# Turning gated operands and block queries in 32x32 squares on VectorE and through DRAM, instead of on TensorE

## The chip, the cores and the metric

The kernel runs on one core of one Trainium2 chip. The metric is device time in microseconds (us) of one execution; lower is better. TensorE (PE in the profile) multiplies matrices, VectorE (DVE), ScalarE (ACT) and GpSimd (POOL) work on elements, and SyncE (SP) issues nearly all DMA transfers. SBUF and PSUM are the memories on the chip, DRAM the one beside it.

## The reference

One decoder block in float32 over 256 tokens of width 1024. A projection gives the inputs of two groups of four heads each: gated linear attention (GLA) and block attention (MoBA, called block attention here). Both are followed by one output projection, a SwiGLU network and a norm.

```python
h = rms_norm(x, norm1_gain[l])
proj = h @ w_in[l]                    # gq, gk, gv, gr, g_low, mq, mk, mv
...
q_dec = q * jnp.exp(b); k_inv = k * jnp.exp(-b)        # b: running sum of log gates
a = jnp.where(causal, jnp.einsum('bhncd,bhnsd->bhncs', q_dec, k_inv), 0.0)
...                                   # intra-chunk part, state part
q_m = rotary(to_heads(mq, MOBA_HEADS), positions)
k_m = rotary(to_heads(mk, MOBA_HEADS), positions)
o_moba = moba_attention(q_m, k_m, to_heads(mv, MOBA_HEADS))
x = x + jnp.concatenate([o_gla, o_moba], axis=-1) @ w_out[l]
h = rms_norm(x, norm2_gain[l])
x = x + (jax.nn.silu(h @ w_ffn_gate[l]) * (h @ w_ffn_up[l])) @ w_ffn_down[l]
return rms_norm(x, final_norm_gain)
```

With 256 tokens there is one key block, so block attention is causal attention here. Scores need queries and keys with the head dimension on the partitions, while the projection delivers them with tokens on the partitions: they have to be turned.

## The kernel before

**Units.** The weights come in units of 128x2048 float32 (1 MB, two DMAs of 512 KB on SP's queue) into a ring of three raw buffers. Each unit is split into a high and a low part: ScalarE's `split` rounds raw to `w_hi` (L858), VectorE's `split` subtracts (`w_lo`, L1072). TensorE multiplies three times (hi*hi, lo*hi, hi*lo; L471 to L473), 24 matrix products of 512 columns for each unit. Units 0 to 11 are the input projection, two for each block of columns: 0, 1 GLA queries and keys; 2, 3 block queries; 4, 5 block keys; 6, 7 block values; 8, 9 GLA values; 10, 11 the output gate. Units 12 to 15 are the output projection, the rest the network.

**What sets the order.** Everything is written out by hand, engine by engine, with semaphores; every engine runs its own list in order. SP loads unit u into the raw buffer only when VectorE has split unit u - 3 (`raw_free`), so VectorE's splits pace the loads. ScalarE's `split(u)` waits for the landing of unit u, VectorE's for ScalarE's, TensorE for both (`unit_ready`).

**The small steps.** TensorE's list puts the attention steps between the halves of the units (`midway`) or behind them (`after`):

```python
midway = {2: [logits], 7: [lambda: moba_transposed(1)],
          9: [probs_transposed], 10: [moba_outputs, gla_updates], 11: [lambda: heads_transposed(0, (3, 0)), gla_outputs]}
after = {3: [cumulate], 4: [gla_transposed],
         6: [gla_scores, lambda: moba_transposed(0)], 7: [moba_scores]}
```

- `gla_transposed` (L576, reading `reuse_c`): ten 128x128 transposes of the gated operands after unit 4. ScalarE copies PSUM to `qdT`, `kiT`, `qcT` (L926 to L930), VectorE the other half of `qdT` (L1191). `gla_scores` (L626) after unit 6 reads them.
- `moba_transposed(0)` and `(1)` (L576, reading `reuse_e`): eight transposes each, of the rotated block queries (after unit 6) and keys (in the middle of unit 7). Copies: ScalarE L935 and L940, VectorE L1194 and L1208. `moba_scores` (L636, L640) after unit 7 reads them.
- VectorE: gates multiply the operands (L1180 to L1185), `split(6)`, `split(7)`, `rotate(0)` (six operations, L1170 to L1175), `split(8)`, a copy, `rotate(1)`, a copy, `split(9)`, four masked copies of GLA scores (L1203), a copy, `split(10)`, the row maxima of the block scores (L1212 to L1222), `split(11)`, `split(12)`.
- ScalarE: `take_block(1)` (L875, block queries out of PSUM), `split(8)`, three copies, `split(9)`, `take_block(2)` (keys; it overwrites what `rotate(0)` reads, so it waits for `rotated` 1), a copy, `split(10)`, `split(11)`, a copy, `split(12)`, `take_block(3)` (values), the eight exponentials of the softmax (L948), a table load (L951), `split(13)`. `probs_transposed` in the middle of unit 9 waits for the exponentials.

## Time and profile before

| | us |
|---|---|
| median of 3 runs (305.68 to 305.84) | 305.72 |
| the profiled execution's own time | 305.38 |
| its span, first to last instruction | 303.7 |
| PE busy in the span | 296.2 |
| DVE busy | 231.7 |
| ACT busy | 153.7 |

The page gives busy time by engine, the granted clock of TensorE, the chain that ended last, the costliest groups and the DMA issues. In a timeline a line is: start in us, duration in us, engine, line of the kernel, operation, out<-in, size of an operand, count, and in brackets the idle time of the engine before it with what released it. Several like instructions in a row are merged into one line (x8). Durations of neighbours on one engine overlap by some tens of ns, so the step from start to start is what an instruction takes in a row of others. Engine SPq is SyncE's queue of DMA issues.

### The profile page before, as it was taken

Reading aid. Unit: us, or ns where it says so; the run is one execution under the profiler, and the core shown is the slowest. Engines: PE = TensorE matmul, PEld = TensorE weight load, DVE = VectorE, ACT = ScalarE, POOL = GpSimd, SP = SyncE. Lnnn points to the kernel's source line nnn. Section 1 sums busy time; section 2 is a strip of 40 time slices with the busy share of each in tenths; the row PEclk is TensorE's granted clock in tenths of the full one; section 3 lists DMA queues with packets and bytes.
Section 4 is the critical chain, followed back from the end, with each engine's and each line's share of the span. In section 5 each row is a group of like instructions: output and inputs, shape, how many; then the busy total and the mean of one; then the engine's idle time right before and its main releaser. Section 6 shows DMA issues by size and latency. Waiting matters only on the chain.

```text
span 303.7 us, 4006 instructions
## 1 busy us (share of the span) xinstructions
PE 296.2 (98%) x1407; PEld 247.1 (81%) x1407; DVE 231.7 (76%) x375; ACT 153.7 (51%) x189; POOL 21.9 (7%) x42
## 2 busy tenths in 40 slices
PE   8999999999999999999999999999999999999992
PEld 7788888888888888888888888888888888888881
DVE  1999999996487257679797979797878878787155
ACT  2898994699363527326262626262617071713123
POOL 6050100000112001500000000000000000000011
PEclk9999999999999999999999999999999999999998
DMA  7987856337825303914747474747472919030003
GB/s 233 359 294 254 276 200 218 138 141 276 276 86 192 138 2 92 316 77 156 262 158 259 159 255 158 256 163 252 139 276 82 331 34 368 19 133 0 0 2 138
DMA packets 36599, 54.42 MB, mean 179 GB/s; under 512 B 2870, under 2 KB 25962, under 8 KB 36586
## 3 DMA queue, kind: packets, MB, share of 16 engines
q1 hardware_dynamic: 36420, 54.08, 52.1%
q8 instruction: 8, 0.13, 0.2%
q10 hardware_dynamic: 166, 0.17, 0.2%
q14 instruction: 5, 0.04, 0.0%
HBM read 53.19 MB, written 1.05 MB: 179 GB/s over the span
## 4 chain that ended last, share of the span: by engine, by line
PE 94%; DMA 2%; DVE 1%; issue 1%; POOL 1%; ACT 0%; SPq 0%; POOLq 0%; DVEq 0%
PE acc L471 15%; PE acc L473 14%; PE acc L472 14%; PE aux L471 13%; PE aux L472 13%; PE aux L473 13%; PE aux L576 3%; DMA raw<-in_w_in 2%; PE acc L525 1%; PE acc L528 1%; PE acc L531 1%; PE aux L658 1%; DVE x_sb L1285 1%; PE aux L682 1%; PE aux L640 1%
## 5 line engine op out<-in xcount | busy, mean ns | idle before, releaser
L1072 DVE TENSOR_TENSOR w_lo<-raw,w_hi 128x2048 fp32r<-128x2048 f32 x47 | 105.6, 2287 | 11.3 <-ACT w_hi L858 11.2
L858 ACT CAST w_hi<-raw 128x2048 fp32r<-128x2048 f32 x47 | 87.7, 1907 | 6.9 <-DMA raw<-in_w_out 3.3
L471 PE MATMUL aux<-w_hi,aT_hi 128*128 128x512 f32 (+1 forms) x180 | 69.8, 388 | 0.0
L473 PE MATMUL aux<-w_hi,aT_lo 128*128 128x512 f32 (+1 forms) x180 | 69.6, 387 | 0.0
L472 PE MATMUL aux<-w_lo,aT_hi 128*128 128x512 f32 (+1 forms) x180 | 69.6, 387 | 0.0
L1321 DVE STREAM_TRANSPOSE reuse_c<-reuse_c 32x128 f32<-32x128 f32 x160 | 48.4, 303 | 2.4
L471 PE MATMUL acc<-w_hi,aT_hi 128*128 128x512 f32 x118 | 47.3, 401 | 0.0
L473 PE MATMUL acc<-w_hi,aT_lo 128*128 128x512 f32 x118 | 46.1, 391 | 0.0
L472 PE MATMUL acc<-w_lo,aT_hi 128*128 128x512 f32 x118 | 46.0, 390 | 0.0
L473 PEld LDWEIGHTS aux<-w_hi,aT_lo 128*128 128x128 f32 x180 | 33.8, 188 | 6.9
L471 PEld LDWEIGHTS aux<-w_hi,aT_hi 128*128 128x128 f32 x180 | 33.8, 188 | 6.9
L472 PEld LDWEIGHTS aux<-w_lo,aT_hi 128*128 128x128 f32 x180 | 33.8, 188 | 6.7
L1015 ACT CAST pT_hi<-reuse_c 128x512 fp32r<-128x512 f32 x10 | 6.2, 621 | 64.7 <-DVE reuse_c L1321 64.7
L471 PE MATMUL acc<-w_hi,pT_hi 128*128 128x512 f32 x80 | 31.2, 390 | 0.0
L473 PE MATMUL acc<-w_hi,pT_lo 128*128 128x512 f32 x80 | 31.1, 389 | 0.0
L472 PE MATMUL acc<-w_lo,pT_hi 128*128 128x512 f32 x80 | 31.1, 389 | 0.0
L1002 ACT ACTIVATE reuse_c<-aux,rstd 128x256 f32<-128x256 f32 x22 | 10.2, 472 | 32.4 <-PE aux L473 32.3
L473 PEld LDWEIGHTS acc<-w_hi,aT_lo 128*128 128x128 f32 x118 | 22.2, 188 | 4.8
L471 PEld LDWEIGHTS acc<-w_hi,aT_hi 128*128 128x128 f32 x118 | 22.2, 188 | 4.4 <-issue 0.2
L472 PEld LDWEIGHTS acc<-w_lo,aT_hi 128*128 128x128 f32 x118 | 22.2, 188 | 4.3
L1311 DVE SCALAR_TENSOR_TENSOR reuse_c<-aux,rstd,reuse_c 128x256 f32<-128x256 f32 x22 | 10.2, 480 | 13.2 <-ACT reuse_c L1002 13.2
L473 PEld LDWEIGHTS acc<-w_hi,pT_lo 128*128 128x128 f32 x80 | 15.0, 188 | 3.2
(199 smaller groups left out, 272.1 us busy)
## 6 DMA issues: line engine op xcount, KB each, us to landing
raw<-in_w_ffn_gate SPq DMA_DIRECT2D x22, 512.0 KB, 4.2
raw<-in_w_ffn_up SPq DMA_DIRECT2D x22, 512.0 KB, 5.3
raw<-in_w_ffn_down SPq DMA_DIRECT2D x22, 512.0 KB, 5.7
raw<-in_w_in SPq DMA_DIRECT2D x20, 512.0 KB, 4.7
raw<-in_w_out SPq DMA_DIRECT2D x8, 512.0 KB, 3.9
raw<-in_w_in SPq DMA_DIRECT2D x8, 256.0 KB, 6.2
x_sb<-in_x SPq DMA_DIRECT2D x2, 512.0 KB, 3.9
reuse_a<-in_final_norm_gain SPq DMA_DIRECT2D x1, 512.0 KB, 4.3
```

Of the source, the lines that this page charges most:

```text
L471: nc.tensor.matmul(dst, left_hi[:, k, tok], right_hi, start=first, stop=False)
L472: nc.tensor.matmul(dst, left_hi[:, k, tok], right_lo, start=False, stop=False)
L473: return nc.tensor.matmul(dst, left_lo[:, k, tok], right_hi, start=False, stop=last)
L525: nc.tensor.matmul(acc[:, t, :], aT_hi[:, k, toks[t]], right_hi, start=k == 0, stop=False)
L528: nc.tensor.matmul(acc[:, t, :], aT_hi[:, k, toks[t]], right_lo, start=False, stop=False)
L576: last = nc.tensor.transpose(aux[:, bank, n * P:(n + 1) * P], src, ident[:, :])
L858: nc.scalar.copy(w_hi[:, slot % RING, :], raw[:, slot % RAW, :]).then_inc(hi_ready, 1)
L1002: nc.scalar.activation(silu_g[:, t, :], aux[:, GATE_UP_BANKS[parity][t], 0:FF], ACT.Silu, scale=rstd[:, 1, t:t + 1]).then_inc(silu_ready, 1)
L1015: nc.scalar.copy(dst, src.rearrange("p (k s) -> p k s", k=2)).then_inc(hiddenT_hi_ready, 1)
L1072: nc.vector.tensor_tensor(w_lo[:, slot % RING, :], raw[:, slot % RAW, :], w_hi[:, slot % RING, :].bitcast(f32), ALU.subtract).then_inc(lo_ ...
L1311: nc.vector.scalar_tensor_tensor(out=hidden[:, t, :], in0=aux[:, GATE_UP_BANKS[parity][t], FF:2 * FF], scalar=rstd[:, 1, t:t + 1], in1=sil ...
L1321: last = nc.vector.transpose(cols[SQUARE * c:SQUARE * (c + 1), :, :, g, :], rows[SQUARE * g:SQUARE * (g + 1), :, :, c, :])
```

## The change

The ten transposes of the GLA operands and the eight of the block queries leave TensorE; the eight of the block keys stay. In their place VectorE turns all 32x32 squares of a group in one instruction (`nc.vector.transpose`: 128x1280 for GLA, 128x1024 for the block queries) into a buffer of squares. SP writes the squares to a DRAM scratch (one DMA each, 640 KB and 512 KB), waits for it to land, and reads them back with four DMAs each, one for each group of 32 partitions, so that the squares arrive at their place. GLA queries are used where they land (`gla_columns`); ScalarE copies the other GLA operands to `kT` and the block queries to `mT_q`, so that they lie in contiguous columns. The orders change too: on VectorE the turn of the GLA operands comes before `split(6)`, the turn of the block queries and `rotate(1)` before `split(8)`, and `split(9)` behind the masked copies and the copy of the keys; on ScalarE `take_block(2)` comes before `split(9)`, the copy to `kT` behind it, the copy to `mT_q` behind `split(10)`; on SP the waits and DMAs of the two moves stand between the loads of units 8 and 11. The semaphores' declarations and two like lists are left out of the diff.

```diff
@@ -52,7 +52,9 @@
 SQUARE = 32
-QUADS = 4
+QUADS = P // SQUARE
+GLA_TILES = 4 * PAIRS + PAIRS
+MOBA_TILES = T * HEADS
 X2T_BANKS = (0, 3, 1, 2)
...
@@ -139,9 +141,8 @@
         lowT = sb("lowT", [SEQ])
-        qdT = sb("qdT", [PAIRS, 2, SEQ])
-        kiT = sb("kiT", [PAIRS, SEQ])
-        qcT = sb("qcT", [PAIRS, P])
+        gla_columns = sb("gla_columns", [QUADS, GLA_TILES, SQUARE])
+        kT = sb("kT", [3 * PAIRS, P])
         state = sb("state", [HEADS, DV])
...
@@ -178,7 +179,9 @@
         q_mid, k_mid = (reuse_c[:, 512 * i:512 * i + 512].rearrange("p (t n) -> p t n", t=T) for i in range(2))
-        k_end, q_cum = (reuse_c[:, 1024 + QK * i:1024 + QK * (i + 1)] for i in range(2))
+        q_cum, k_end = (reuse_c[:, 1024 + QK * i:1024 + QK * (i + 1)] for i in range(2))
+        gla_rows = reuse_c[:, 0:GLA_TILES * P].rearrange("p (n c i) -> p c n i", c=QUADS, i=SQUARE)
+        gla_squares = reuse_f[:, 0:GLA_TILES * P].rearrange("p (c n i) -> p c n i", c=QUADS, i=SQUARE)
         squares = reuse_c[:, 0:1024]
...
@@ -190,7 +193,11 @@
         s_1 = reuse_e[:, 512:1536].rearrange("p (h k) -> p h k", h=HEADS)
-        mT = reuse_f[:, :].rearrange("p (w h s) -> p w h s", w=2, h=HEADS)
+        m_columns = reuse_f[:, 0:1024].rearrange("p (c n i) -> p c n i", c=QUADS, i=SQUARE)
+        mT_q = reuse_a[:, :].rearrange("p (t h s) -> p t h s", t=T, h=HEADS)
+        mT_k = reuse_f[:, 1024:2048].rearrange("p (h s) -> p h s", h=HEADS)
+        m_rows = reuse_e[:, 0:1024].rearrange("p (n c i) -> p c n i", c=QUADS, i=SQUARE)
+        m_squares = reuse_c[:, 0:1024].rearrange("p (c n i) -> p c n i", c=QUADS, i=SQUARE)
         probT = reuse_f[:, 0:1536].rearrange("p (b h q) -> p b h q", b=3, h=HEADS)
...
@@ -301,6 +313,9 @@
+        gla_moves = nc.dram_tensor("gla_moves", (P, QUADS, GLA_TILES * SQUARE), f32).ap()
+        m_moves = nc.dram_tensor("m_moves", (P, QUADS, MOBA_TILES * SQUARE), f32).ap()
+
         block = ctx.enter_context(nc.Block())
@@ -355,9 +370,29 @@
             sp.dma_start(gate_bias, b_gate.to_broadcast([P, QK])).then_inc(bias_loaded, 16)
-            for u in range(RAW, IN_UNITS):
-                raw_free(u)
-                rows_unit(u % RAW, w_in[0], (u % 2) * 4 * P, 4, BLOCKS[u // 2], 512)
+            def in_units(lo, hi):
+                for u in range(lo, hi):
+                    raw_free(u)
+                    rows_unit(u % RAW, w_in[0], (u % 2) * 4 * P, 4, BLOCKS[u // 2], 512)
+
+            def squares_out(ready, n, moves, squares, moved):
+                sp.wait_ge(ready, n)
+                sp.dma_start(moves, squares.rearrange("p c n i -> p c (n i)")).then_inc(moved, 16)
+
+            def columns_back(moved, moves, columns, landed):
+                sp.wait_ge(moved, 16)
+                for c in range(QUADS):
+                    sp.dma_start(columns[SQUARE * c:SQUARE * (c + 1)].rearrange("p g n i -> p g (n i)"),
+                                 moves[:, c, :].rearrange("(g j) n -> j g n", g=QUADS)).then_inc(landed, 16)
+
+            in_units(RAW, 9)
+            squares_out(gla_squares_ready, 1, gla_moves, gla_squares, gla_moved_out)
+            in_units(9, 10)
+            columns_back(gla_moved_out, gla_moves, gla_columns, gla_columns_back)
+            in_units(10, 11)
+            squares_out(m_squares_ready, 1, m_moves, m_squares, m_moved_out)
+            columns_back(m_moved_out, m_moves, m_columns, m_columns_back)
+            in_units(11, IN_UNITS)
             for n in range(OUT_UNITS):
...
@@ -405,7 +440,6 @@
             nc.gpsimd.memset(one[:, :], 1.0)
-            nc.gpsimd.memset(qdT[:, :, :, :], 0.0)
             nc.gpsimd.memset(state[:, :, :], 0.0)
...
@@ -590,55 +624,44 @@
                 for t, tri in enumerate((tri_rest, tri_cum)):
-                    cols = slice(t * QK, (t + 1) * QK)
-                    nc.tensor.matmul(aux[:, 3, cols], tri[:, :], log_hi[:, cols], start=True, stop=False)
-                    last = nc.tensor.matmul(aux[:, 3, cols], tri[:, :], log_lo[:, cols], start=False, stop=True)
+                    cols, dst = slice(t * QK, (t + 1) * QK), slice((1 - t) * QK, (2 - t) * QK)
+                    nc.tensor.matmul(aux[:, 3, dst], tri[:, :], log_hi[:, cols], start=True, stop=False)
+                    last = nc.tensor.matmul(aux[:, 3, dst], tri[:, :], log_lo[:, cols], start=False, stop=True)
                 last.then_inc(cum_in_psum, 1)
-            def gla_transposed():
-                pe.wait_ge(gla_ops_ready, 3)
-                for bank, src in ((1, q_mid), (2, k_mid)):
-                    transposes(bank, [src[:, t, pair * P:(pair + 1) * P] for pair in range(PAIRS)
-                                      for t in range(T)]).then_inc(glaT_in_psum, 1)
-                transposes(0, [q_cum[:, pair * P:(pair + 1) * P] for pair in range(PAIRS)]).then_inc(glaT_in_psum, 1)
-
-            def moba_transposed(which):
-                pe.wait_ge(rotated, which + 1)
-                if which == 0:
-                    pe.wait_ge(glaT_by_act, 3)
-                else:
-                    pe.wait_ge(mT_by_act, 1)
-                    pe.wait_ge(mT_by_dve, 1)
+            def moba_k_transposed():
+                pe.wait_ge(rotated, 2)
                 for n, bank in enumerate((3, 0)):
-                    transposes(bank, [m_rot[:, which, t, h, :] for h in (2 * n, 2 * n + 1)
+                    transposes(bank, [m_rot[:, 1, t, h, :] for h in (2 * n, 2 * n + 1)
                                       for t in range(T)]).then_inc(mT_in_psum, 1)
...
-                pe.wait_ge(glaT_by_act, 2)
-                pe.wait_ge(glaT_by_dve, 1)
+                pe.wait_ge(gla_columns_back, 16 * QUADS)
+                pe.wait_ge(kT_ready, 1)
                 for t in range(T):
-                    tok = slice(t * P, (t + 1) * P)
                     for pair in range(PAIRS):
...
                             rows = slice(par * DK, (par + 1) * DK)
-                            last = nc.tensor.matmul(aux[:, 1 + par, col:col + P], kiT[rows, pair, tok],
-                                                    qdT[rows, pair, par, tok], start=True, stop=True)
+                            n = t * PAIRS + pair
+                            last = nc.tensor.matmul(aux[:, 1 + par, col:col + P], kT[rows, n, :],
+                                                    gla_columns[rows, :, n, :], start=True, stop=True)
                 last.then_inc(a_in_psum, 1)
...
-                pe.wait_ge(mT_by_act, 2)
-                pe.wait_ge(mT_by_dve, 2)
+                pe.wait_ge(mT_q_ready, 1)
+                pe.wait_ge(mT_by_act, 1)
+                pe.wait_ge(mT_by_dve, 1)
                 pe.wait_ge(a_ready, 2)
                 for h in range(HEADS):
-                    last = nc.tensor.matmul(aux[:, 1, h * P:(h + 1) * P], mT[:, 0, h, 0:P], mT[:, 1, h, 0:P],
+                    last = nc.tensor.matmul(aux[:, 1, h * P:(h + 1) * P], mT_q[:, 0, h, :], mT_k[:, h, 0:P],
                                             start=True, stop=True)
...
                 for h in range(HEADS):
-                    last = nc.tensor.matmul(aux[:, 2 + h // 2, (h % 2) * SEQ:(h % 2 + 1) * SEQ], mT[:, 0, h, P:SEQ],
-                                            mT[:, 1, h, :], start=True, stop=True)
+                    last = nc.tensor.matmul(aux[:, 2 + h // 2, (h % 2) * SEQ:(h % 2 + 1) * SEQ], mT_q[:, 1, h, :],
+                                            mT_k[:, h, :], start=True, stop=True)
                     if h % 2:
...
@@ -682,7 +705,7 @@
                         if t:
-                            last = nc.tensor.matmul(aux[:, 1 + t, cols], qcT[:, h // 2, :], state[:, h, :],
+                            last = nc.tensor.matmul(aux[:, 1 + t, cols], kT[:, 2 * PAIRS + h // 2, :], state[:, h, :],
                                                     start=False, stop=True)
...
@@ -765,10 +788,9 @@
-            midway = {2: [logits], 7: [lambda: moba_transposed(1)],
+            midway = {2: [logits], 7: [moba_k_transposed],
                       9: [probs_transposed], 10: [moba_outputs, gla_updates], 11: [lambda: heads_transposed(0, (3, 0)), gla_outputs]}
-            after = {3: [cumulate], 4: [gla_transposed],
-                     6: [gla_scores, lambda: moba_transposed(0)], 7: [moba_scores]}
+            after = {3: [cumulate], 6: [gla_scores], 7: [moba_scores]}
             for k in range(KC):
...
@@ -922,22 +944,20 @@
             split(8)
-            act.wait_ge(glaT_in_psum, 1)
-            nc.scalar.copy(qdT[0:DK, :, 0, :], aux[0:DK, 1, :].rearrange("p (a s) -> p a s", a=PAIRS)).then_inc(glaT_by_act, 1)
-            act.wait_ge(glaT_in_psum, 2)
-            nc.scalar.copy(kiT[:, :, :], aux[:, 2, :].rearrange("p (a s) -> p a s", a=PAIRS)).then_inc(glaT_by_act, 1)
-            act.wait_ge(glaT_in_psum, 3)
-            nc.scalar.copy(qcT[:, :, :], aux[:, 0, 0:PAIRS * P].rearrange("p (a s) -> p a s", a=PAIRS)).then_inc(glaT_by_act, 1)
-            split(9)
             act.wait_ge(rotated, 1)
             take_block(2, m_flat)
+            split(9)
+            act.wait_ge(gla_columns_back, 16 * QUADS)
+            nc.scalar.copy(kT[:, :, :].rearrange("p n (g i) -> p n g i", g=QUADS),
+                           gla_columns[:, :, 2 * PAIRS:GLA_TILES, :].rearrange("p g n i -> p n g i")).then_inc(kT_ready, 1)
+            split(10)
+            act.wait_ge(m_columns_back, 16 * QUADS)
+            nc.scalar.copy(mT_q.rearrange("p t h (g i) -> p (t h) g i", g=QUADS),
+                           m_columns.rearrange("p g n i -> p n g i")).then_inc(mT_q_ready, 1)
+            act.wait_ge(rotated, 2)
             act.wait_ge(mT_in_psum, 1)
-            nc.scalar.copy(mT[:, 0, 0:2, :], aux[:, 3, :].rearrange("p (h s) -> p h s", h=2)).then_inc(mT_by_act, 1)
-            split(10)
+            nc.scalar.copy(mT_k[:, 0:2, :], aux[:, 3, :].rearrange("p (h s) -> p h s", h=2)).then_inc(mT_by_act, 1)
             split(11)
-            act.wait_ge(rotated, 2)
-            act.wait_ge(mT_in_psum, 3)
-            nc.scalar.copy(mT[:, 1, 0:2, :], aux[:, 3, :].rearrange("p (h s) -> p h s", h=2)).then_inc(mT_by_act, 1)
             split(12)
...
@@ -1183,16 +1203,15 @@
             nc.vector.tensor_tensor(k_end, gqk[:, 0, QK:2 * QK], k_end, ALU.mult).then_inc(gla_ops_ready, 1)
+            dve.wait_ge(gla_ops_ready, 3)
+            nc.vector.transpose(gla_squares, gla_rows).then_inc(gla_squares_ready, 1)
             split(6)
...
             rotate(0)
+            dve.wait_ge(rotated, 1)
+            nc.vector.transpose(m_squares, m_rows).then_inc(m_squares_ready, 1)
+            rotate(1)
             split(8)
-            dve.wait_ge(glaT_in_psum, 1)
-            nc.vector.tensor_copy(qdT[DK:P, :, 1, :], aux[DK:P, 1, :].rearrange("p (a s) -> p a s", a=PAIRS)).then_inc(glaT_by_dve, 1)
-            rotate(1)
-            dve.wait_ge(mT_in_psum, 2)
-            nc.vector.tensor_copy(mT[:, 0, 2:4, :], aux[:, 0, :].rearrange("p (h s) -> p h s", h=2)).then_inc(mT_by_dve, 1)
-            split(9)
...
@@ -1204,8 +1223,9 @@
                 last.then_inc(a_ready, 1)
-            dve.wait_ge(mT_in_psum, 4)
-            nc.vector.tensor_copy(mT[:, 1, 2:4, :], aux[:, 0, :].rearrange("p (h s) -> p h s", h=2)).then_inc(mT_by_dve, 1)
+            dve.wait_ge(mT_in_psum, 2)
+            nc.vector.tensor_copy(mT_k[:, 2:4, :], aux[:, 0, :].rearrange("p (h s) -> p h s", h=2)).then_inc(mT_by_dve, 1)
+            split(9)
             split(10)
...
```

## Rows read from the trace of the kernel before

**Rows 1.** The page: busy time by engine, and the chain that ended last.

```profile
PE 296.2 (98%) x1407; PEld 247.1 (81%) x1407; DVE 231.7 (76%) x375; ACT 153.7 (51%) x189; POOL 21.9 (7%) x42
...
PE 94%; DMA 2%; DVE 1%; issue 1%; POOL 1%; ACT 0%; SPq 0%; POOLq 0%; DVEq 0%
```

**Rows 2.** Timeline of TensorE around unit 4's end: start, us, instruction.

```profile
39.26 0.40 PE L473 MATMUL acc<-w_hi,aT_lo 128*128 128x512 f32 x1
39.50 1.25 PE L576 MATMUL aux<-ident,reuse_c 128*128 128x128 f32 x10
40.51 0.48 PE L471 MATMUL acc<-w_hi,aT_hi 128*128 128x512 f32 x1
40.82 0.39 PE L472 MATMUL acc<-w_lo,aT_hi 128*128 128x512 f32 x1
```

**Rows 3.** Timeline of TensorE from the GLA scores to unit 9's middle.

```profile
51.59 1.16 PE L626 MATMUL aux<-qdT,kiT 64*128 64x128 f32 x16
52.69 1.09 PE L576 MATMUL aux<-ident,reuse_e 128*128 128x128 f32 x8
53.53 0.48 PE L471 MATMUL acc<-w_hi,aT_hi 128*128 128x512 f32 x1
...
56.40 1.04 PE L576 MATMUL aux<-ident,reuse_e 128*128 128x128 f32 x8
...
60.01 1.05 PE L636 MATMUL aux<-reuse_f 128*128 128x128 f32 x8
...
62.44 0.58 PE L471 MATMUL acc<-w_hi,aT_hi 128*128 128x512 f32 x1
...
70.83 1.47 PE L576 MATMUL aux<-ident,reuse_e 128*128 128x128 f32 x12
```

**Rows 4.** Timeline of VectorE, 37 to 66 us.

```profile
37.76 4.49 DVE L1072 TENSOR_TENSOR w_lo<-raw,w_hi 128x2048 fp32r<-128x2048 f32 x2
42.18 0.69 DVE L1170 TENSOR_TENSOR reuse_e<-reuse_d,cos_t 128x512 f32<-128x512 f32 x1
...
46.18 2.28 DVE L1072 TENSOR_TENSOR w_lo<-raw,w_hi 128x2048 fp32r<-128x2048 f32 x1
...
54.42 2.28 DVE L1072 TENSOR_TENSOR w_lo<-raw,w_hi 128x2048 fp32r<-128x2048 f32 x1
56.62 1.44 DVE L1203 COPY_PREDICATED reuse_b<-gla_mask,aux 128x256 f32<-128x256 int32 x4
57.95 0.68 DVE L1208 COPY reuse_f<-aux 128x512 f32<-128x512 f32 x1
...
61.10 0.69 DVE L1212 TENSOR_TENSOR reuse_e<-aux,causal 128x512 f32<-128x512 f32 x1 [0.27 <-PE aux L636]
...
65.27 4.49 DVE L1072 TENSOR_TENSOR w_lo<-raw,w_hi 128x2048 fp32r<-128x2048 f32 x2
```

**Rows 5.** Timeline of ScalarE, 47 to 68 us.

```profile
47.40 1.26 ACT L875 ACTIVATE reuse_d<-acc,rstd 128x512 f32<-128x512 f32 x2
...
61.39 1.90 ACT L858 CAST w_hi<-raw 128x2048 fp32r<-128x2048 f32 x1 [3.33 <-DMA raw<-in_w_out]
...
64.35 0.40 ACT L948 ACTIVATE reuse_e<-reuse_e,neg_max 128x128 f32<-128x128 f32 x1
...
67.98 1.28 ACT L951 ACT_TABLE_LOAD   x1
```

**Rows 6.** Timeline of SyncE's DMA issues: the load of unit 12.

```profile
56.73 0.82 SPq L320 DMA_DIRECT2D raw<-in_w_out  x2
```

**Rows 7.** Page: the 32x32 transposes. Columns: busy us, mean ns.

```profile
L1321 DVE STREAM_TRANSPOSE reuse_c<-reuse_c 32x128 f32<-32x128 f32 x160 | 48.4, 303 | 2.4
```

**Rows 8.** Groups by shape on VectorE, 30 to 75 us.

```profile
L1116 DVE SCALAR_TENSOR_TENSOR reuse_e<-reuse_e 128x128 f32<-128x128 f32 x3 | 0.9, 293 | 0.1
```

**Rows 9.** DMA issues: count, KB each, median us from issue to landing.

```profile
out<-reuse_e ACTq DMA_DIRECT2D x1, 160.0 KB, 2.3
```

**Rows 10.** Busy time, clock, DMA share and GB/s of one microsecond.

```profile
43.00:44.00 1.00, 1.00 (x6) 0.83 (x5) 1.00 (x2) 1.00 (x2) 0.00 (x0) 1.00 1.04 401
```

More of the change, by code:

```diff
@@ L253, in build_block @@
         gla_ops_ready = sem("gla_ops_ready")
-        glaT_in_psum = sem("glaT_in_psum")
-        glaT_by_act = sem("glaT_by_act")
-        glaT_by_dve = sem("glaT_by_dve")
+        gla_squares_ready = sem("gla_squares_ready")
+        gla_moved_out = sem("gla_moved_out")
+        gla_columns_back = sem("gla_columns_back")
+        kT_ready = sem("kT_ready")
+        m_squares_ready = sem("m_squares_ready")
+        m_moved_out = sem("m_moved_out")
+        m_columns_back = sem("m_columns_back")
+        mT_q_ready = sem("mT_q_ready")
         mT_in_psum = sem("mT_in_psum")
```

## The prediction, made before the changed kernel was run

> **What bounds the kernel now.** I read the page first: TensorE is busy for 98% of the span, and 94% of the chain that ended last is TensorE's [rows 1]. So TensorE's own list is the critical path, and any transpose taken from it counts in full unless something new makes TensorE wait. Then I read TensorE's timeline through the attention steps, from start to start [rows 2, 3]: there is no gap. Then the timelines of the engines that feed it. VectorE runs without a pause from 37.76 us through `split(9)` to the row maxima [rows 4]: at this place the second engine is full too, and its splits release SP's loads. ScalarE's exponentials run from 64.35 to 67.98 us [rows 5], and TensorE transposes their result at 70.83 us [rows 3]: 2.85 us of slack. That slack, and how much work the change puts on VectorE ahead of `split(9)`, is what the forecast turns on.
>
> **What is removed from TensorE.** The ten transposes after unit 4 start at 39.50 us and unit 5 at 40.51 us, and the first product behind them takes 0.31 us to the next start instead of 0.23: 1.01 + 0.08 = 1.09 us [rows 2]. The eight transposes of the block queries take 53.53 - 52.69 = 0.84 us [rows 3]. Together 1.93 us, from 18 of 26 transposes; the eight of the keys stay. The scores themselves read other tiles at the same sizes: nothing.
>
> **VectorE's new list.** A transpose of 128 elements per partition takes 303 ns [rows 7]. No row shows one of 1280. Lower value: an ordinary operation takes 293 ns at 128 elements [rows 8] and 2280 at 2048 [rows 4], so 1.04 ns for each further element; 303 + 1152 x 1.04 = 1.50 us for GLA and 303 + 896 x 1.04 = 1.24 us for the block queries. Upper value: ten and eight times 303 ns, 3.03 and 2.42 us. I take the lower: a slope twice as steep would leave some 40 ns of fixed cost for the 128-element transpose, and its duration is within 10 ns of the ordinary operation's. Nothing supports less than the slope of the other operations, so there is no end below. The Trainium skill ("Vector Engine (DVE) Microarchitecture Reference", section 3.8) states of the transpose mode that it is "Pipelined to sustain one element per cycle per lane"; by that the two together are about the 2.74 us taken, against 5.45 us by the upper value, and the row of 303 ns agrees with it as far as it goes.
>
> The list then runs so, with steps from rows 4. The GLA turn 37.76 to 39.26. `split(6)`, `split(7)` take 4.42 (37.76 to 42.18): to 43.68. `rotate(0)` takes 4.00 (42.18 to 46.18): to 47.68, plus about 0.1 until its end is seen. The turn of the queries: to 49.0. `rotate(1)` needs the keys that ScalarE takes meanwhile (47.8 + 1.26 [rows 5] = 49.1): 49.15 to 53.15. `split(8)`, 2.21 (half of 4.42): to 55.36. The masked copies, 1.33 (56.62 to 57.95): to 56.70. The keys' copy, 0.6: to 57.30, if TensorE has the keys turned by 56.7 (below: just). `split(9)`, 56.62 - 54.42 = 2.2 to the next start, its result 2.28 after its start: 59.58. Before, that result stood at 56.70. So the release of unit 12's load is 2.88 us later: two turns (2.74) and two steps put ahead (1.93), less two copies and an idle half microsecond that go.
>
> **First new wait: GLA scores.** On ScalarE `take_block(2)` waits for `rotate(0)`, until 47.8 us, and `split(9)` is queued behind it, and the copy to `kT` behind that. One split and one take take 64.35 - 61.39 = 2.96 us [rows 5]: 50.8. The copy of 768 columns: between 0.63 us for 512 (half of 1.26) and 1.90 for 2048 [rows 5] lies 0.84. `kT` stands at 51.65, TensorE sees it at 51.7. Without a wait it would start these scores at 51.59 - 1.09 = 50.50 us [rows 2, 3]. The wait costs 1.20 us. Behind it on TensorE stands everything.
>
> The move through DRAM is hidden behind this, by my sum: a DMA of 160 KB takes 2.3 us to landing [rows 9], and a busy queue moves 401 GB/s [rows 10]. Write of 640 KB from 39.3: 2.3 + 0.49 MB / 401 GB/s = 3.5, landed 42.8. Unit 9's load is issued at 41.6, after `split(6)`, and lands 4.66 us later (as unit 12's: issued 56.73 [rows 6], used 61.39 [rows 5]), 46.3; the four reads stand behind its bytes: 0.655 MB more, 47.9. Needed at 50.8. Unit 10's load follows on the queue, lands at about 50.5, needed at 51.65.
>
> **Second new wait: the exponentials.** From the GLA scores' start TensorE reaches, without the queries' transposes, the middle of unit 7 after 1.10 + 2.87 = 3.97 us, the block scores after another 3.61, the middle of unit 9 after another 10.82 (60.01 to 70.83) [rows 3]. From 51.70: keys turned at 55.7 to 56.5, block scores at 59.28, middle of unit 9 at 70.10. For the block scores: the squares of the queries are ready at 49.05, their write is behind unit 10's load and lands at some 52.3, four reads (0.41 us each to issue, half of 0.82 [rows 6]) land at 52.3 + 1.2 + 2.3 = 55.8, ScalarE's copies of 1024 columns (1.05) and of the keys (0.5) end at 57.4: no wait. But unit 12's load is 2.88 us later, and ScalarE takes its list in order: `split(12)` at 61.39 + 2.88 = 64.27, then `take_block(3)` and the exponentials as before, which end at 67.98 + 2.88 = 70.86. The row maxima are not later than that (VectorE starts them at 61.7 after `split(10)`, 0.6 later than the 61.10 of before [rows 4]). TensorE at 70.10 waits 0.77 us.
>
> **Sum.** -1.93 + 1.20 + 0.77 = +0.04 us: TensorE stands in the middle of unit 9 at 70.87, before 70.83. From there it is bound by its own products as before: the loads of units 13 to 17 are issued 1 to 3 us later, and ScalarE's waits there are for TensorE, which covers them; if that cover were gone, up to those 1 to 3 us would come on top. The profiled execution's own time is 305.38 us, so 305.4; the median of the runs is 0.34 higher, and for it I forecast 305.8.
>
> **Rivals.**
>
> *As it is meant: only the transposes go.* 305.72 - 1.93 = 303.8. It asks ScalarE to have `kT` at 50.5 and VectorE to be no later. The order in the lists speaks against it. In between, if the first wait stands and the second does not: 305.72 - 0.73 = 305.0. For that VectorE or a load must be 0.8 us earlier than summed; loads vary by that much.
>
> *The turns run at 303 ns for each 128 elements.* VectorE is 1.53 + 1.18 = 2.71 us later at `split(9)`, so are the exponentials: 305.8 + 2.7 = 308.5. For: no row shows a long transpose, and these do not overlap like other operations. Against: the fixed cost it would leave. It decides from the first tenths, since the second wait passes everything on.
>
> *The reads back are slow, and the block scores wait for them.* Each read fills 32 partitions only, in pieces of 1024 or 1280 bytes; the loads fill 128. No row shows such a read. At 401 GB/s it is hidden (above), at half the rate still: GLA lands at 49.6, the queries at 57 to 58, and they cost something only past 60.05 - 1.55 = 58.5 (70.87 - 10.82, less ScalarE's copies). At a quarter, 100 GB/s, GLA lands at 52.9, 2.1 us too late, unit 10 behind it, and the queries at about 64: TensorE in the middle of unit 9 at some 76, that is 311. So this ends slower than before, from a rate of some 180 GB/s downward. The Trainium skill ("SBUF — State Buffer", section "Door 1: The DMA port swizzle") says that 32 partitions reach 8 of 16 ports, with 189 GB/s measured there at 1 MiB, and that two transfers for different halves do not add up. By that rule the queries land near 58, at the very edge, and the time is 305.8 to 306.5.
>
> *TensorE's clock.* Two gaps of about 1 us appear in a TensorE that had none here; the granted clock is 1.00 in this stretch [rows 10]. If it falls behind a gap, each microsecond at the lower level costs half a microsecond. I give it little.
>
> **Chances.** Forecast (both waits, +0.04, give or take 0.5): 0.50. As meant, or with the first wait alone: 0.13. Slow turns: 0.12. Slow reads: 0.19. Clock or another new wait: 0.06. The measurement tells 0.2%, 0.6 us, from no change. Same: 0.46 of the forecast, 0.03 of slow reads that just touch, 0.02 of the case with the first wait alone: 0.51. Faster: 0.11 of the second and 0.01 of the forecast, 0.12. Slower: the rest, 0.37. Range: 305.0, where only the first wait stands, to 308.6, where the turns are slow; outside lie the full gain and reads at under 150 GB/s, together under 2 in 10. The likeliest case's own range is 305.3 to 306.3.
>
> **What would show it.** TensorE idle ahead of `gla_scores`, 1.2 us, released by ScalarE's copy to `kT` (if by a DMA: slow reads), and ahead of `probs_transposed`, 0.8 us, released by ScalarE's exponentials (L948). The two turns at 1.5 and 1.24 us. `take_block(2)` at 47.8, unit 12's load issued at 59.6. The block scores not waiting. The forecast is wrong if TensorE waits for `mT_q`, if the turns take 3 us, or if either wait is missing.

## The result, and the profile after

| | us |
|---|---|
| the changed kernel, median of 11 runs (306.32 to 307.74) | 306.87 |
| the kernel before, median of the 11 runs of that comparison (305.09 to 306.1) | 305.48 |
| ratio after / before, 95% interval | 1.0046, 1.0033 to 1.0058 |
| the profiled execution's own time, after (before 305.38) | 306.37 |
| its span (before 303.7) | 304.6 |

The change makes the kernel 1.4 us slower, clear of its noise. That is inside the stated range (305.0 to 308.6), but above the 305.8 of the likeliest case and outside that case's own range (305.3 to 306.3). TensorE does less and waits more. The first line is the page's; then who TensorE waited for in the whole span (us in total, times, longest).

```profile
PE 294.6 (97%) x1389; PEld 245.3 (81%) x1389; DVE 233.1 (77%) x375; ACT 153.7 (50%) x187; POOL 21.3 (7%) x41
```

```profile
PE aux L648 <- ACT kT L951: 1.4, 1, 1.4
PE acc L522 <- DVE w_lo L1116: 1.2, 1, 1.2
PE aux L659 <- ACT reuse_a L955: 0.9, 1, 0.9
```

Busy time of TensorE fell from 296.2 [rows 1] to 294.6 us; the 18 transposes that left were 1.93 us from start to start. Two waits are new behind unit 0: 1.4 us for ScalarE's copy to `kT`, ahead of the GLA scores, and 0.9 us for ScalarE's copy of the block queries, ahead of the block scores. In the timeline of TensorE:

```profile
50.51 0.39 PE L507 MATMUL acc<-w_hi,aT_lo 128*128 128x512 f32 x1
52.27 1.16 PE L648 MATMUL aux<-gla_columns,kT 64*128 64x128 f32 x16 [1.37 <-ACT kT L951]
...
56.24 1.04 PE L610 MATMUL aux<-ident,reuse_e 128*128 128x128 f32 x8
...
59.62 0.39 PE L507 MATMUL acc<-w_hi,aT_lo 128*128 128x512 f32 x1
60.91 1.13 PE L659 MATMUL aux<-reuse_f,reuse_a 128*128 128x128 f32 x8 [0.90 <-ACT reuse_a L955]
...
71.83 1.47 PE L610 MATMUL aux<-ident,reuse_e 128*128 128x128 f32 x12
```

The last product before the first gap starts at 50.51 and takes 0.23 to the next start, so the first gap is 52.27 - 50.74 = 1.53 us from start to start; the second is 60.91 - 59.85 = 1.06. Against rows 3, the middle of unit 9 stands at 71.83 instead of 70.83. The account of this 1.00 us:

- The first product of unit 0 starts at 8.17 instead of 7.81, and the whole 0.36 us is still there at 19 us. Of the 13 kernels profiled here all but the kernel before start it between 7.93 and 8.47, `e_before_exps`, which moves nothing, at 8.15. So this belongs to the run and not to the change.
- The transposes that are gone: -1.93.
- The gaps: +1.53 and +1.06, less 0.09 that stood at the first place before.
- Small steps: +0.07.

There is no gap ahead of `probs_transposed`, and the own times of the two profiled executions differ by that same 0.99 us: nothing is gained or lost behind unit 9.

The 11 runs of the changed kernel fall in two groups by the mean granted clock of each. Seven have 0.994 to 0.998 and take 306.32 to 306.97 us (median 306.54, the profiled one among them). Four have 0.988 or 0.989 and take 307.38 to 307.74.

VectorE, then ScalarE, against rows 4 and 5:

```profile
38.13 1.51 DVE L1207 STREAM_TRANSPOSE reuse_f<-reuse_c 128x1280 f32<-128x1280 f32 x1
...
48.04 1.25 DVE L1212 STREAM_TRANSPOSE reuse_c<-reuse_e 128x1024 f32<-128x1024 f32 x1
...
57.31 0.69 DVE L1227 COPY reuse_f<-aux 128x512 f32<-128x512 f32 x1 [0.34 <-PE aux L610]
57.92 4.49 DVE L1092 TENSOR_TENSOR w_lo<-raw,w_hi 128x2048 fp32r<-128x2048 f32 x2
```

```profile
48.04 1.27 ACT L897 ACTIVATE reuse_d<-acc,rstd 128x512 f32<-128x512 f32 x2 [3.72 <-DVE reuse_e L1195]
49.20 1.91 ACT L880 CAST w_hi<-raw 128x2048 fp32r<-128x2048 f32 x1
51.29 0.83 ACT L951 COPY kT<-gla_columns 128x768 f32<-128x768 f32 x1 [0.18 <-DMA gla_columns<-gla_moves]
...
59.27 1.05 ACT L955 COPY reuse_a<-reuse_f 128x1024 f32<-128x1024 f32 x1 [3.70 <-DMA reuse_f<-m_moves]
...
64.92 1.91 ACT L880 CAST w_hi<-raw 128x2048 fp32r<-128x2048 f32 x1 [1.13 <-DMA raw<-in_w_out]
...
71.52 1.28 ACT L971 ACT_TABLE_LOAD   x1
```

VectorE's turns of the squares take 1.51 and 1.25 us. `take_block(2)` waits 3.72 us for `rotate(0)`; the copy to `kT` (L951) waits for `split(9)` and then 0.18 us more for the GLA reads. The copy of the queries (L955) waits 3.70 us for the reads of `m_moves`. The exponentials (L968) end at 71.5, just ahead of TensorE's 71.83. SyncE's issues, and with them the median us from issue to landing:

```profile
49.31 0.34 SPq L380 DMA_DIRECT2D m_moves<-reuse_c  x1
54.92 1.75 SPq L385 DMA_DIRECT2D reuse_f<-m_moves  x4
...
60.23 0.82 SPq L335 DMA_DIRECT2D raw<-in_w_out  x2
```

```profile
gla_moves<-reuse_f SPq DMA_DIRECT2D x1, 640.0 KB, 2.9
gla_columns<-gla_moves SPq DMA_DIRECT2D x4, 160.0 KB, 5.7
m_moves<-reuse_c SPq DMA_DIRECT2D x1, 512.0 KB, 5.6
reuse_f<-m_moves SPq DMA_DIRECT2D x4, 128.0 KB, 2.9
```

The GLA reads one by one (durations of the issues in ns, then first and last start, then the time to landing):

```profile
L385 SPq DMA_DIRECT2D gla_columns<-gla_moves x4: 438/454/479, 42.8 to 44.3; - x4
...
DMA to landing us min/median/max: 5.4/5.7/7.0
```

The four stand behind unit 9's load and land 5.4 to 7.0 us after issue, the last at 44.3 + 7.0 = 51.3. Unit 10's load stands behind them, the write of the queries (issued at 49.31, 5.6 us to landing) behind that. So the queries' reads are issued at 54.92, not at 52.3. Busy share and rate of the DMA engines (last two columns):

```profile
44.00:46.00 2.00, 2.00 (x11) 1.65 (x10) 1.97 (x5) 0.32 (x1) 0.00 (x0) 1.00 1.04 400
46.00:48.00 2.00, 2.00 (x10) 1.67 (x9) 1.93 (x3) 0.00 (x0) 0.00 (x0) 1.00 1.11 255
47.00:48.00 1.00, 1.00 (x6) 0.82 (x5) 0.97 (x2) 0.00 (x0) 0.00 (x0) 1.00 1.10 206
48.00:49.00 1.00, 1.00 (x6) 0.83 (x5) 0.97 (x2) 0.96 (x2) 0.00 (x0) 1.00 1.16 221
48.00:50.00 2.00, 2.00 (x10) 1.67 (x9) 1.91 (x4) 1.96 (x3) 0.00 (x0) 1.00 1.10 240
50.00:52.00 2.00, 0.90 (x4) 0.39 (x3) 1.93 (x5) 1.82 (x2) 0.00 (x0) 1.00 1.07 386
```

From 46 to 50 us the engines are fully busy (share 1.1) and move 240 to 255 GB/s: mostly the GLA reads, with some bytes of their neighbours at both ends. In the two microseconds from 47 to 49, where all but 23 of 365 packets are smaller than 2 KB, as those of the reads are, it is 206 and 221 GB/s. Before and after them, with about the same share, unit loads move 386 to 400. These are the reads that fill 32 partitions each.

### The profile page after: what moved, and what is told of

Read it like the earlier page. It is cut to its first block, busy times and chain, and to the rows that moved or that the text cites. A ratio compares the mean times of both kernels' runs of the same rounds, so it can differ in the third digit from the quotient of the medians.

```text
span 304.6 us, 3976 instructions
## 1 busy us (share of the span) xinstructions
PE 294.6 (97%) x1389; PEld 245.3 (81%) x1389; DVE 233.1 (77%) x375; ACT 153.7 (50%) x187; POOL 21.3 (7%) x41
## 4 chain that ended last, share of the span: by engine, by line
PE 82%; DVE 5%; DMA 5%; ACT 3%; issue 2%; SPq 1%; POOL 1%; POOLq 0%; DVEq 0%; ACTq 0%
PE aux L507 13%; PE aux L506 13%; PE aux L505 13%; PE acc L505 11%; PE acc L507 11%; PE acc L506 11%; DMA raw<-in_w_in 2%; DMA m_moves<-reuse_c 2%; PE aux L610 2%; PE acc L559 1%; PE acc L562 1%; PE acc L565 1%; ACT w_hi L880 1%; DMA reuse_f<-m_moves 1%; PE aux L681 1%
## 5 line engine op out<-in xcount | busy, mean ns | idle before, releaser
L506 PEld LDWEIGHTS acc<-w_lo,pT_hi 128*128 128x128 f32 x80 | 15.0, 188 | 3.1
```

Of the source, the lines that this page charges most:

```text
L506: nc.tensor.matmul(dst, left_hi[:, k, tok], right_lo, start=False, stop=False)
```

## The experiments

All ratios are to the kernel before, run beside. For each kernel there is what it does, what was expected of it before it ran, and what came out. Where a difference in us is given by the ratio, it is the ratio times the time of the kernel before.

**One part alone.** `e_gla_only` moves the GLA operands and turns the queries on TensorE; `e_queries_only` the reverse. Their edits put back the other kernel's lines. Of these only TensorE's table is shown; `e_gla_only` also gives VectorE back the order `split(8)`, `rotate(1)`, `split(9)`, and `e_queries_only` gives ScalarE back `split(9)` ahead of `take_block(2)`:

```diff
 # e_gla_only
-after = {3: [cumulate], 6: [gla_scores], 7: [moba_scores]}
+after = {3: [cumulate], 6: [gla_scores, lambda: moba_transposed(0)], 7: [moba_scores]}
 # e_queries_only
+after = {3: [cumulate], 4: [gla_transposed], 6: [gla_scores], 7: [moba_scores]}
```

> Only the GLA operands move through VectorE and DRAM; the block queries are turned by TensorE and copied out as before. Theory (the loss is made of waits in series: ScalarE's list and the landing of the GLA reads make the GLA scores late, the query reads make the block scores late): TensorE saves 1.1 us and waits some 1.3 us ahead of the GLA scores, nothing ahead of the block scores, so +0.2 us against the kernel before, 0.0 to +0.5. Rival (VectorE's time is what costs: each turn of 1.2 to 1.5 us reaches the end through the splits): a bit over half of the whole change's +1.4 us, +0.7 or more.

> Only the block queries move through VectorE and DRAM; the GLA operands are turned by TensorE as before. Theory (the query reads were late in the changed kernel because their write stood behind unit 10's load, and that behind the slow GLA reads): without the GLA move unit 10's load is out of the way, the query reads land near 55 us, no wait ahead of the block scores, TensorE keeps its 0.84 us except for 0.0 to 0.2 at the exponentials: -0.7 us against the kernel before. Rival (a move through DRAM is too long in itself for this gap, or VectorE's list costs as in the whole change): 0.0 to +0.7 us, with TensorE waiting for the copy of the queries or for the exponentials.

`e_gla_only`: 306.24 us, ratio 1.0036 (1.0018 to 1.0053), so 0.5 us slower by the medians and 1.1 by the ratio. TensorE waits 1.5 us ahead of the GLA scores and nowhere else behind unit 0. That is the theory's mechanism, a little dearer than its price; by the time alone the rival's 0.7 us or more would fit as well. Nine of its twelve runs take 305.95 to 306.43; the other three take 308.0 to 308.2, and these three have the lowest granted clock (0.988 to 0.990, the nine 0.994 to 0.998). `e_queries_only`: 305.89 us, 1.0012 (1.0002 to 1.0021). The theory's -0.7 failed. The write of the queries landed 2.7 us after issue and there was no wait ahead of the block scores, as it said; but TensorE waited ahead of `probs_transposed`:

```profile
PE aux L604 <- ACT reuse_e L972: 0.6, 1, 0.6
```

The GLA move alone costs more than it saves, and the queries' move alone meets a limit that the changed kernel hides.

**The queue ahead of the query reads.**

```diff
 # e_m_first, SP; on ScalarE the copies of queries and keys before split(10)
-            in_units(10, 11)
             squares_out(m_squares_ready, 1, m_moves, m_squares, m_moved_out)
             columns_back(m_moved_out, m_moves, m_columns, m_columns_back)
+            in_units(10, 11)
```

> The changed kernel, but on SP the move of the block queries stands before unit 10's load, and on ScalarE the copies of queries and keys before split(10). Theory (the queue order makes the query reads late): they land near 56 us instead of 59, the wait ahead of the block scores goes, and a third limit shows, the exponentials, with a wait of 0.0 to 0.5 us: 0.6 to 1.0 us faster than the changed kernel, +0.4 to +0.8 against the kernel before. Rival (the reads are late because of their own latency): wait ahead of the block scores still 0.5 us or more, +1.0 or more.

306.59 us, 1.0032 (1.0016 to 1.0047), which is +1.0 by the ratio and a little more than the +0.4 to +0.8 expected. The write now lands 2.6 us after issue, the copy of the queries starts at 56.07 instead of 59.27, and the wait ahead of the block scores is gone. In its place:

```profile
PE aux L648 <- ACT kT L951: 1.1, 1, 1.1
PE aux L610 <- ACT reuse_e L968: 1.0, 1, 1.0
```

The exponentials are 1.0 us late, twice what was expected, and nearly all that was won is given back. Here unit 10 comes later too, and `split(10)` of VectorE with it (it waits 1.42 us for ScalarE).

**Both moves ahead of the loads, and then the third limit too.**

```diff
 # e_gm_first: e_m_first, and on SP
+            columns_back(gla_moved_out, gla_moves, gla_columns, gla_columns_back)
             in_units(9, 10)
-            columns_back(gla_moved_out, gla_moves, gla_columns, gla_columns_back)
 # on ScalarE
             take_block(2, m_flat)
-            split(9)
             (copy to kT)
+            split(9)
 # e_exps_first: the changed kernel, and on ScalarE
-            split(12)
             take_block(3, mv)
             (eight exponentials)
+            split(12)
 # on VectorE
-            split(10)
             (row maxima)
+            split(10)
 # e_all: e_gm_first and e_exps_first together
```

> The changed kernel with one reorder: on ScalarE take_block(3) and the exponentials stand before split(12), on VectorE the row maxima before split(10). It takes away the third limit (unit 12's load, released late by VectorE's split(9), stands ahead of the exponentials) and leaves the waits ahead of the GLA scores (1.4 us) and the block scores (0.9 us). Theory (three limits in series, each hidden by the one before): no gain here, since the exponentials were in time in the changed kernel: within 0.3 us of it, +1.1 to +1.5 us against the kernel before. Rival (VectorE's list is what the change costs): 0.5 us or more faster than the changed kernel.

> The changed kernel with both moves put ahead of loads: on SP the GLA reads before unit 9's load and the block queries' move before unit 10's; on ScalarE the copy to kT before split(9), the copies of queries and keys before split(10). Theory: both waits ahead of scores go (GLA reads land near 48 us, the query reads near 56), TensorE is 1.9 us ahead at unit 8 and gives nearly all of it back ahead of probs_transposed, in one wait of 1.6 to 2.2 us for the exponentials, since unit 12's load is not a bit earlier: +0.0 to +0.6 us against the kernel before. Rival (the waits ahead of the scores were the whole loss): 0.5 us or more faster than the kernel before.

> Both reorders together: the moves ahead of the loads, and the exponentials ahead of split(12) with the maxima ahead of split(10). Theory (the three limits are all there is): no wait of TensorE over 0.3 us from unit 5 to unit 11, the 1.93 us of transposes come through: -1.9 us against the kernel before, -2.2 to -1.3. Rival (a further limit, in VectorE's 2.7 us of turns or in the later loads of units 13 to 17): -1.0 to +0.5, with a new wait behind unit 9.

`e_exps_first`: 306.69 us, 1.0034 (1.0022 to 1.0046), and the same two waits (1.5 and 0.9): within 0.2 us of the changed kernel, no gain while the other limits stand. `e_gm_first`: 307.83 us, 1.0052 (1.0028 to 1.0075), runs from 305.38 to 309.27. Both waits ahead of scores are gone, and one of 2.5 us stands ahead of `probs_transposed`, a little over the 1.6 to 2.2 expected. That gives +0.6 us, as forecast; measured is +1.6 by the ratio, and the profiled run took 308.01. Here too the runs split by the granted clock: five at 0.996 to 0.999 take 305.38 to 306.54 us (median 306.19, 0.5 above the kernel before), seven at 0.990 to 0.993 take 307.78 to 309.27. The waits, and the windows around the gap (PE busy is the second number, the granted clock the third from the end):

```profile
PE aux L610 <- ACT reuse_e L968: 2.5, 1, 2.5
```

```profile
70.00:71.00 1.00, 0.00 (x0) 0.00 (x0) 1.00 (x1) 1.00 (x5) 0.00 (x0) 1.00 0.29 61
71.00:72.00 1.00, 0.19 (x1) 0.20 (x2) 0.94 (x1) 0.98 (x5) 0.00 (x0) 0.85 0.87 319
72.00:73.00 1.00, 1.00 (x6) 1.00 (x6) 0.00 (x0) 1.00 (x1) 0.00 (x0) 0.50 1.04 422
73.00:74.00 1.00, 1.00 (x7) 1.00 (x6) 0.00 (x0) 0.99 (x2) 0.00 (x0) 0.50 1.02 401
74.00:75.00 1.00, 1.00 (x5) 0.90 (x5) 0.34 (x1) 1.00 (x2) 0.00 (x0) 0.50 0.97 389
75.00:76.00 1.00, 1.00 (x6) 0.83 (x5) 1.00 (x2) 1.00 (x3) 0.00 (x0) 0.95 0.95 377
```

`e_all`: 304.10 us (304.06 to 304.36), 0.9949 (0.9936 to 0.9962): 1.6 us faster than the kernel before, 2.8 faster than the changed one. Run once more:

> The same kernel as e_all, to see it on another chip or hour beside the control. Theory: -1.4 to -1.9 us against the kernel before, no wait of TensorE over 0.3 us from unit 5 to unit 11. Rival (its narrow spread was luck): under 1.0 us faster, or runs that scatter by over 1 us as in the changed kernel.

304.06 us, 0.9941 (0.9928 to 0.9954). TensorE's waits in `e_all`, and VectorE's list where the maxima now stand:

```profile
PE acc L522 <- DVE w_lo L1116: 1.2, 1, 1.2
PE aux L610 <- ACT reuse_e L967: 0.2, 1, 0.2
```

```profile
59.74 0.68 DVE L1231 TENSOR_TENSOR reuse_e<-aux,causal 128x512 f32<-128x512 f32 x1
...
63.91 4.49 DVE L1092 TENSOR_TENSOR w_lo<-raw,w_hi 128x2048 fp32r<-128x2048 f32 x2
```

The middle of unit 9 stands at 69.74 us. That is 1.09 us before the kernel before, though this run's first product came at 8.47, 0.66 later (of which 0.45 is left at 19 us). None of the eleven runs of the two comparisons has a mean granted clock under 0.994. VectorE still makes both turns and the scratch is still written and read; nothing of it is seen in the time once what they delay is not what TensorE wants next.

**The reorder by itself, and with one move.**

The two edits of `e_exps_first`, put into the kernel before and into `e_queries_only`:

> The kernel before with the reorder alone: exponentials ahead of split(12), row maxima ahead of split(10); all 26 transposes on TensorE. Theory (TensorE has no wait there, so there is nothing to gain): 0.0 us, within 0.3. Rival (the reorder gains by itself, and e_all's 1.6 us are partly its own): -0.4 us or more.

> Only the block queries move (as in e_queries_only), and the exponentials stand ahead of split(12), the row maxima ahead of split(10). Theory (in e_queries_only the exponentials were the one limit, a wait of 0.56 us): that wait goes, and the 0.84 us of the eight transposes come through: -0.8 us against the kernel before, -1.1 to -0.5. Rival (VectorE's turn or DRAM traffic costs somewhere else): -0.2 to +0.5.

`e_before_exps`: 305.47 us, 0.9996 (0.9987 to 1.0005): nothing. `e_queries_exps`: 304.62 us, 0.9965 (0.9954 to 0.9976), which is 0.9 us faster than the kernel before by the medians and 1.1 by the ratio (0.7 to 1.4); the 0.84 us of the transposes lie inside. The wait ahead of `probs_transposed` is gone. The reorder is worth nothing where TensorE does not wait, 1.3 us by the medians with the queries' move (305.89 to 304.62, two comparisons), and it is needed for the whole. Of the 1.3 us the profiled executions show 0.8 (305.61 and 304.85), about what the wait cost from start to start (0.7); the rest is not explained.

**The rate of the reads.** `e_full_reads` lets each read fill 128 partitions; `e_one_read` lets four writes do the ordering, and reads once.

```diff
 # e_full_reads
-                    sp.dma_start(columns[SQUARE * c:SQUARE * (c + 1)]...,
-                                 moves[:, c, :].rearrange("(g j) n -> j g n", g=QUADS))
+                    sp.dma_start(columns[:, g]...,
+                                 moves[SQUARE * g:SQUARE * (g + 1)].rearrange("j c n -> c j n"))
 # e_one_read, moves now (c, j, g, n)
+                    sp.dma_start(moves[:, :, g, :].rearrange("c j n -> j c n"), squares[SQUARE * g:SQUARE * (g + 1)]...)
+                sp.dma_start(columns..., moves.rearrange("c j g n -> (c j) (g n)"))
```

> The changed kernel, but each of the four reads back fills all 128 partitions (one slice of 256 or 320 columns) instead of 32 partitions. Same bytes, same size of piece. Theory (reads into 32 partitions run at about half rate, some 210 GB/s in the microseconds of the GLA reads): the GLA reads land 1.3 to 1.6 us earlier, the query write as much earlier, the wait of 0.9 us ahead of the block scores goes or shrinks to 0.2; the wait ahead of the GLA scores shrinks by only 0.2, since ScalarE's list holds the copy until 51 us: 0.6 to 0.9 us faster than the changed kernel, +0.5 to +0.8 against the kernel before. Rival (the reads are slow for another reason, the small pieces or DRAM itself): landing times and waits as in the changed kernel, +1.4.

> The changed kernel, but the squares are put in order by the writes: four writes, each from 32 partitions, outermost size 32, and one read that fills 128 partitions in pieces of 4 or 5 KB. Theory (transfers that touch 32 partitions run at half rate): the write of the GLA squares takes 5 us instead of 2.9, the one read runs at about 400 GB/s and lands near 49.5 us instead of 51.3; the block queries land near 58 instead of 59.2: wait ahead of the GLA scores as before or 0.2 less (ScalarE's list), ahead of the block scores 0.0 to 0.4: 0.4 to 0.9 us faster than the changed kernel. Rival (small pieces or the reading of DRAM set the rate): the writes take under 4 us.

`e_full_reads`: 318.51 us, 1.0417 (1.0395 to 1.0439): a clear miss of both. TensorE waits 6.4 us ahead of the GLA scores and 4.0 ahead of the block scores.

```profile
46.00:48.00 2.00, 2.00 (x11) 1.65 (x10) 1.90 (x4) 0.07 (x1) 0.00 (x0) 1.00 0.28 69
...
54.00:56.00 2.00, 0.00 (x0) 0.00 (x0) 1.51 (x1) 0.00 (x0) 0.00 (x0) 0.61 0.27 96
56.00:58.00 2.00, 0.82 (x8) 0.85 (x10) 0.00 (x0) 0.83 (x1) 0.00 (x0) 0.50 0.27 105
...
62.00:64.00 2.00, 2.00 (x14) 1.75 (x14) 0.00 (x0) 0.00 (x0) 0.00 (x0) 1.00 0.25 88
```

While hardly anything but the GLA reads runs (46 to 48 us; 93 of 107 packets are under 2 KB), 0.28 of the engines' time is busy and 69 GB/s move. While the queries' reads run (62 to 64), it is 0.25 and 88 GB/s. From 56 to 58 us the packets are of 2 KB again, so these are bytes of the load and the write behind the reads, still at a share of 0.27. All of this is a quarter of the engines or a little more. The outermost dimension of these reads is 4, that of all others 32 or more; that they are spread by that dimension over four engines fits the share, but no run varied it alone. So this kernel could not tell the rate of 128 partitions with all engines at work.

One estimate can be drawn from it. The rate divided by the share is what the engines would move if they were always busy: 88 / 0.25 = some 350 GB/s for these reads of the queries, against 261 / 1.05 = 249 in the changed kernel (57 to 58 us), with the same pieces of 1024 bytes; for the GLA reads, with pieces of 1280 bytes, 69 / 0.28 = some 246 against (206 + 221) / (1.10 + 1.16) = 189. So small pieces alone do not explain the slow reads. That only four engines or so were at work at once is a difference that these runs do not take away.

`e_one_read`: 306.69 us, 1.0051 (1.0026 to 1.0077), runs from 306.16 to 311.02. The GLA writes took 2.8 us each to landing (median), the four together from 39.54 to 43.96, where the read is issued: 4.4 us against 2.9 for the one write, between the theory's 5 and the rival's under 4. But the fourth write is issued only at 40.9, 1.4 us behind the first, so the 4.4 us are mostly issue and landing, and tell little of the rate. The windows of the writes (41 to 44), and of the read with unit 9's last bytes ahead of it (46 to 48):

```profile
41.00:42.00 1.00, 1.00 (x6) 0.82 (x5) 1.00 (x2) 0.99 (x3) 0.00 (x0) 1.00 0.90 183
42.00:43.00 1.00, 1.00 (x6) 0.83 (x5) 1.00 (x1) 1.00 (x2) 0.00 (x0) 1.00 1.00 292
43.00:44.00 1.00, 1.00 (x6) 0.84 (x5) 1.00 (x2) 1.00 (x1) 0.00 (x0) 1.00 0.90 141
...
46.00:47.00 1.00, 1.00 (x6) 0.81 (x5) 0.97 (x2) 0.00 (x0) 0.00 (x0) 1.00 1.12 372
47.00:48.00 1.00, 1.00 (x6) 0.84 (x5) 0.93 (x3) 0.09 (x1) 0.00 (x0) 1.00 0.93 378
```

The wait ahead of the block scores is gone, that ahead of the GLA scores is 1.1. But unit 11's load landed late in the profiled run, and the exponentials were 3.0 us late behind it; at 309.69 us it is one of the four long runs of nine. The expected 0.4 to 0.9 us did not come. As to the rate: a read that fills 128 partitions runs at 378 GB/s (47 to 48 us) where four of 32 ran at 206 to 221, and the microseconds with the writes out of 32 show 141 to 292, where the one write out of 128 moved 420 (changed kernel, 41 to 42 us). The pieces differ here too (the one read's are 5120 bytes, those of the four 1280), so this pair does not separate them; with the estimate above the evidence leans to the 32 partitions, and it is not shown.

## Why the prediction came out as it did

The number fell inside the range, and in part this was luck. The upper end of 308.6 stood for slow turns, which did not come. By the signs that the prediction had named itself, its likeliest case was wrong: TensorE waited for `mT_q`, and the wait for the exponentials was missing. It had also given 0.51 to "no change" (within 0.6 us), and 0.37 to slower, which came.

**What bounds the kernel, and what the transposes are worth.** Right: `e_all` keeps 1.6 and 1.8 of 1.93 us by its two ratios.

**VectorE's turns.** Right: 1.50 and 1.24 summed, 1.51 and 1.25 measured. The upper value (3.03 and 2.42) is ruled out.

**VectorE's list to unit 12's load.** Right: `split(9)` from 57.92 against 57.30 summed, of which 0.36 is the run's start and 0.34 VectorE's wait for the keys, one step behind the longer first wait; unit 12's load issued at 60.23 against 59.61.

**The first wait.** Place and cause right, the size 1.53 against 1.20. `take_block(2)` came when it should (48.04, less 0.36 of start, against 47.8); the scores came 0.21 us later than 51.70 + 0.36, 0.18 of it the GLA reads, and 0.09 is how the gap is counted. The step "the four reads stand behind its bytes: 0.655 MB more, 47.9" was wrong by 3.4 us (the last landed at 51.3); that it cost only 0.2 is ScalarE's order.

**The block scores.** This is the step that failed: "ScalarE's copies of 1024 columns (1.05) and of the keys (0.5) end at 57.4: no wait". The reads landed at 59.2, not 55.8, and the wait was 1.06 us. Two sizes were off together. The write of the queries landed 2.6 us late (54.9, not 52.3), since unit 10's load and the GLA reads stood ahead of it in the same queue, and its reads took 4.3 us from the first issue instead of 3.5. I had put the GLA reads at 401 GB/s, and they ran at 206 to 221; for their 0.655 MB that is some 1.4 us of the 2.6, and 0.36 is the run's start. The rest stays open. `e_m_first` shows what the queue does: without unit 10's load ahead, the write lands in 2.6 us and the wait is gone. The rival of slow reads had named the mechanism, a wait of the block scores, with 305.8 to 306.5 us where they just touch; but it had put the queries at 57 to 58, and had said that the end is later only "from a rate of some 180 GB/s downward", and both were too kind: at 206 to 221 the reads landed at 59.2 and the wait was there. The Trainium skill ("SBUF — State Buffer", section "Door 1: The DMA port swizzle") has 189 GB/s for 32 partitions at 1 MiB; the trace has 206 to 221 with a full share, nearer to that rule than to the 401 that the sum used.

**The second wait.** It was there, but hidden: at 71.5 the exponentials were as late as forecast (70.86, 0.36 of start and 0.3 of the same wait for the keys), and TensorE, held at the block scores, came 0.3 us after them. `e_m_first` (1.0 us), `e_queries_only` (0.56) and `e_gm_first` (2.5) uncover it, and `e_exps_first` shows that removing it alone is worth nothing. So the waits do not add: where the sum had 0.77 ahead of the exponentials, 1.06 ahead of the block scores stood in its place. What the forecast missed of the profiled difference is then 0.3 in the first wait, 0.3 in the second, and 0.36 of start.

**The medians.** The profiled runs differ by 0.99 us, of which 0.36 is start; the medians by 1.4. The granted clock accounts for most of the rest: the seven runs of the changed kernel at 0.994 and above have a median of 306.54, 1.06 above the kernel before, and the four at 0.988 and 0.989 are 0.9 us longer (median 307.48) and lift the median of all to 306.87. In the comparisons for which the clocks of the kernel before are on record (75 runs), it never shows less than 0.993. The end of this text compares the kernels with and without gaps. What stays open is why the clock fell in those four runs and not in the seven, and where in them; none of the four is the profiled one.

**The clock.** "I give it little" was right for the profiled run, where the granted clock stayed at 1.00 across both gaps. It was not right for the kernel: four of its 11 runs lost clock, as did three of twelve of `e_gla_only`, whose only new gap is 1.5 us. For longer gaps it is dearer, see the end.

## What to carry to other kernels

Work that leaves the bound engine comes back as waits in series, and each hides the next: sum the arrival at every place where the bound engine asks for something, and move all of them, or the gain is nil. In lists kept in order, put what the bound engine wants next ahead of splits and loads that it wants later; that, not the cost of the turns, made the same work 1.4 us slower or 1.6 us faster. In one DMA queue a slow transfer delays everything issued behind it, so price its bytes at the rate of its own shape.

## What the runs showed of the hardware

In the profiled run of the changed kernel TensorE's granted clock stayed at 1.00 across gaps of 1.06 and 1.53 us. Four of the other ten runs had a lower mean (0.988 and 0.989, the rest 0.994 to 0.998) and took 0.9 us longer; so such gaps are perhaps not always free. That the gaps are the cause is not shown run by run, but 105 runs of four kernels without a gap of over 0.3 us behind unit 0 (the kernel before, `e_before_exps`, `e_queries_exps`, `e_all`) never have less than 0.993, and the other kernels with gaps of 0.9 to 1.5 us do: three of twelve runs of `e_gla_only`, one of `e_m_first` and four of `e_exps_first` are at 0.988 to 0.991.

With longer gaps the clock fell to the lower of its two levels, 0.50 of 2.4 GHz, in all three profiled kernels that have one:

- `e_gm_first`, gap of 2.47 us: low from 71.7 to 75.1 us, starting as the gap ended. By the windows shown this costs 0.15 + 3 x 0.5 + 0.05 = 1.7 us. The profiled run bears that out: its middle of unit 9 stands at 71.81, 0.98 us behind the kernel before, and its own time is 2.63 us behind (308.01 against 305.38). Its seven runs with the lower mean clock take 1.8 us more than the five others (medians 308.01 and 306.19).
- `e_full_reads`, gap of 6.4 us: low from 54.4, still inside the gap, to 61.3. Behind its second gap, of 4.0 us, it is low again, from 71.5 to 74.9.
- `e_one_read`, gap of 3.0 us that ended at 73.5: low only from 75, with TensorE at work again, to 78.3.

A 32x32 transpose on VectorE of 128 partitions takes 1.25 us for 1024 elements and 1.51 for 1280. Beside the 0.303 us for 128 elements [rows 7] that is 1.05 to 1.06 ns for each further element, close to the 1.04 of the ordinary float32 operations there (293 ns for 128 elements [rows 8], 2.28 us for 2048 [rows 4]).
